# A gated FFN in seven products per tile: where its sums, its modulation rows and its kept stream are handled

## The reference, cut to what matters

```
h = rmsnorm(x, norm_ffn_g)
g = dwconv(h @ w_gate, conv_ffn_w)          # 2816 columns = 22 tiles of 128, 3 taps
v = h @ w_up
x = x + (silu(g) * v) @ w_down              # "output products"
x = rmsnorm(x, norm_final_g)
# second block: 64 columns of 128 values from the vector c
shift, scale, gate = split(silu(c) @ ada_w + ada_b, 3)      # twice, and once in two parts
h = rmsnorm(x, g) * (1 + scale) + shift
```

## Time and profile before

| | us |
|---|---|
| median of 3 runs | 2045.7 (2045.27 to 2046.42) |
| the profiled execution | 2045.31 |
| its span | 2043.5 |
| PE busy in the span | 1990.0 (97%) |
| DVE, ACT, POOL busy | 1348.1, 723.8, 1047.7 |

### The profile page before, as it was taken

How to read it: one execution, slowest core, us unless ns; L and a number is a source line. 1 busy time by engine, 2 the same in 40 slices (tenths; PEclk the granted TensorE clock), 3 DMA queues, 4 the chain that set the end, 5 groups by cost and what they waited for, 6 DMA issues and landing times.

```text
span 2043.5 us, 23948 instructions
## 1 busy us (share of the span) xinstructions
PE 1990.0 (97%) x9084; PEld 1634.0 (80%) x9084; DVE 1348.1 (66%) x1822; ACT 723.8 (35%) x1221; POOL 1047.7 (51%) x620
## 2 busy tenths in 40 slices
PE   9999999799999999999999999999999999999998
PEld 7888888577777778888888888888888878777887
DVE  6999678788888865665576454354355381497556
ACT  6323344433334344111154112112112262598112
POOL 4677828689898985211276132132132174365633
PEclk9999999899999999999999999999999999999999
DMA  4231113144545435222111021021021112010202
GB/s 159 73 114 42 52 42 134 61 177 169 191 154 206 145 121 197 83 89 117 42 40 64 31 65 49 32 71 42 31 72 42 31 42 67 11 33 21 67 17 83
DMA packets 54135, 167.56 MB, mean 82 GB/s; under 512 B 6272, under 2 KB 11536, under 8 KB 54032
## 3 DMA queue, kind: packets, MB, share of 16 engines
q1 hardware_dynamic: 41936, 127.94, 18.1%
q10 hardware_dynamic: 12096, 38.23, 5.3%
HBM read 148.30 MB, written 21.00 MB: 83 GB/s over the span
## 4 chain that ended last, share of the span: by engine, by line
PE 71%; POOL 17%; DVE 5%; issue 4%; ACT 3%; DMA 0%; POOLq 0%; DVEq 0%; SPq 0%; ACTq 0%
PE psum L914 20%; PE psum L915 20%; PE psum L916 20%; POOL w_lo L815 2%; POOL w_lo L806 2%; POOL temp L684 2%; POOL second_sum L800 2%; POOL w_lo L785 1%; POOL even_gate_lo L785 1%; ACT probs L1897 1%; POOL w_lo L810 1%; PE psum L1322 1%; POOL w_raw L802 1%; POOL w_raw L794 1%; DVE psum L1972 1%
## 5 line engine op out<-in xcount | busy, mean ns | idle before, releaser
L649 POOL TENSOR_TENSOR w_lo<-w_raw,w_hi 128x1024 fp32r<-128x1024 f32 x131 | 329.9, 2531 | 606.9 <-ACT w_hi L1422 601.6
L914 PE MATMUL psum<-norm_hi,w_hi 128*128 128x512 f32 (+1 forms) x1200 | 464.9, 387 | 0.0
L915 PE MATMUL psum<-norm_lo,w_hi 128*128 128x512 f32 (+1 forms) x1200 | 463.5, 386 | 0.0
L916 PE MATMUL psum<-norm_hi,w_lo 128*128 128x512 f32 (+1 forms) x1200 | 463.5, 386 | 0.0
L914 PEld LDWEIGHTS psum<-norm_hi,w_hi 128*128 128x128 f32 x1200 | 225.3, 188 | 46.1 <-issue 0.2
L915 PEld LDWEIGHTS psum<-norm_lo,w_hi 128*128 128x128 f32 x1200 | 225.4, 188 | 45.5 <-issue 0.2
L916 PEld LDWEIGHTS psum<-norm_hi,w_lo 128*128 128x128 f32 x1200 | 225.3, 188 | 45.4
L2031 DVE SCALAR_TENSOR_TENSOR stream<-psum,mods,stream 128x512 f32<-128x512 f32 x160 | 119.7, 750 | 172.0 <-PE psum L916 172.0
L1422 ACT CAST w_hi<-w_raw 128x1024 fp32r<-128x1024 f32 x114 | 115.9, 1048 | 218.3 <-PE psum L916 143.5
L2368 DVE TENSOR_TENSOR stream<-psum,stream 128x512 f32<-128x512 f32 x176 | 121.6, 691 | 93.8 <-PE psum L916 93.6
L2120 DVE SCALAR_TENSOR_TENSOR psum<-glu,vec,psum 128x1024 f32<-128x1024 f32 x116 | 149.6, 1290 | 4.1
(11 more groups left out here) (317 smaller groups left out, 4289.6 us busy)
## 6 DMA issues: line engine op xcount, KB each, us to landing
w_raw<-in_slabs SPq DMA_DIRECT2D x155, 512.0 KB, 3.3
ada_raw<-in_ada ACTq DMA_DIRECT2D x16, 2048.0 KB, 7.7
even_raw<-in_slabs SPq DMA_DIRECT2D x20, 512.0 KB, 4.0
ffn_y_scratch<-ffn_y SPq DMA_DIRECT2D x18, 512.0 KB, 3.5
sum_raw<-ffn_y_scratch SPq DMA_DIRECT2D x5, 1024.0 KB, 5.0
stream<-in_x SPq DMA_DIRECT2D x8, 512.0 KB, 9.3
stream_scratch<-stream SPq DMA_DIRECT2D x2, 2048.0 KB, 7.2
stream<-stream_scratch SPq DMA_DIRECT2D x2, 2048.0 KB, 12.0
```

What stands on the lines that cost most here:

```text
L649: nc.gpsimd.tensor_tensor(WL[place][:, :], RAW[at % 2][:, :], WH[place][:, :].bitcast(f32), ALU.subtract).then_inc(slab_ready, 1)
L914: nc.tensor.matmul(dst, wh, xh, start=n == 0, stop=False)
L915: nc.tensor.matmul(dst, wh, xl, start=False, stop=False)
L916: last = nc.tensor.matmul(dst, wl, xh, start=False, stop=n == len(terms) - 1)
```

## The change

- **Sums' low parts.** In the sevens POOL keeps `gate_low`, the four `weight_sums` and the low part of the second sum. The low parts of S1 and of S3/S4 (`sum_low`, `last_low`, 128x1024 each) go to DVE. `mixed_part_sum` is gone from POOL.
- **Parts from PSUM.** Three of the four `keep_part` copies are gone; DVE adds each product from its bank: seven adds a turn, each with one PSUM operand, in place of six on DVE and one on POOL.
- **Modulation rows.** 36 rows (18 turns of two) are done in turns 1 to 18, straight into `mods`; the bias is added once at the end. The other 28 are done behind output products: three each in jobs 1 to 8 (behind tiles 2, 7 and 12), four in job 9 (also behind 15). Their loads are issued by ACT inside its loop over jobs. The gains are made in the last job. POOL's `sums(POOL)` and ACT's `weight_his(POOL_SLAB, ...)` now wait for all rows.
- **`back_low`** moves from DVE to POOL, in front of the job's `lows`.
- **Stream normalised in place.** `piece(FFN, m)` is now the stream's own place, so the sums t1 to t4 are differences of its blocks: two on POOL and six on DVE in place of four on POOL and twelve on DVE. The stream is stored in eight pieces of 512 KB beforehand and `scaled` waits for the store of its piece. It comes back in eight loads, in part before the sevens end.
- The raw and gate buffers swap turns: turn 0 uses `RAW` and place 5, odd turns the spare ones. Row slab 0 may be cast a turn earlier (`row_refill`).

```
-ADA_TURNS, ADA_ROWS = 16, 4
+EARLY_TURNS, TURN_ROWS = 18, 2
+LATE_ROWS = NADA - EARLY_TURNS * TURN_ROWS
+LATE_JOBS = (1, 10)
...
-    early = (last + 2, last + 5, last + 7, last + 7, last + 7, last + 7, DOWN_TILE + 16, DOWN_TILE + 32)
+    early = (last - 5, last + 5, last + 7, last + 7, last + 7, last + 7, DOWN_TILE + 16, DOWN_TILE + 32)
...
         def piece(n, m):
+            if n == FFN:
+                return X[:, m % 8, hs(m // 8)]
...
+        def late_rows(job):
+            return [i for i in range(LATE_ROWS) if min(1 + i // 3, LATE_JOBS[1] - 1) == job]
...
             for half in range(2):
-                sp.wait_ge(dve_read, 56 + 8 * half)
-                sp.dma_start(x_scratch[:, :, hs(half)], X[:, :, hs(half)]).then_inc(x_kept, 16)
+                for k in range(0, KT, 2):
+                    sp.wait_ge(dve_read, 48 + 8 * half + k + 2)
+                    sp.dma_start(x_scratch[:, k:k + 2, hs(half)], X[:, k:k + 2, hs(half)]
+                                 ).then_inc(x_moved[(8 * half + k) // 2], 16)
...
+                nc.gpsimd.tensor_tensor(t1_raw(pair), block_of(0, 1, pair), block_of(0, 0, pair), ALU.subtract
+                                        ).then_inc(t1_made, 1)
-            for n in range(SEVENS):
-                last_low_of(n)
-                if n + 1 < SEVENS:
-                    gate_low(n + 1)
-                    weight_sums(n + 1)
-                mixed_part_sum(n)
-                if n + 1 < SEVENS:
-                    sum_lows(n + 1)
-            lows(ROW_SLAB, POOL_SLAB)
+            for n in range(1, SEVENS):
+                gate_low(n)
+                weight_sums(n)
+                second_low(n)
+            for n in range(len(JOBS)):
+                if n > 1:
+                    back_low(n)
+                lows(ROW_SLAB + 2 * n, ROW_SLAB + 2 * n + 2)
             lows(POOL_SLAB, POOL_SLAB + 2)
-            sums(POOL, (f_lo, 4))
+            sums(POOL, (ada_summed, ALL_SUMMED))
...
-                pe.wait_ge(*((part_added, 6 * n) if n else (act_read, 47)))
+                pe.wait_ge(*((part_added, 7 * n) if n else (act_read, 47)))
...
+            gate_silu(0)
             corner_cast(2, 0)
-            corner_cast(4, 0)
-            corner_cast(3, 0)
-            gate_silu(0)
+            corner_cast(2, 1)
             s1_cast(0)
-            s2_cast(0)
-            s34_cast(0)
-            y_cast(0)
             act.wait_ge(tiles, FFN_TILE + 6)
             corner_cast(1, 0)
             corner_cast(1, 1)
-            corner_cast(2, 1)
-            corner_cast(4, 1)
-            corner_cast(3, 1)
+            y_cast(0)
+            s2_cast(0)
...
+            read_second(0)
+            read_second(1)
+            s34_cast(0)
+            corner_cast(4, 0)
+            corner_cast(4, 1)
+            read_second(2)
+            read_second(3)
...
+            def load_late(i):
+                if i < 2:
+                    act.wait_ge(f_mul, FT)
+                else:
+                    act.wait_ge(ada_summed, EARLY_TURNS + i - 1)
+                act.dma_start(ada_late(i), ada_in[EARLY_TURNS * TURN_ROWS + i, :, :]).then_inc(ada_loaded[i % 2], 16)
...
-                for half in range(2):
-                    keep_part(t + 1, body(T[0], half), bank[0])
+                keep_part(t + 1, body(T[0], 1), bank[0])
...
-                act.wait_ge(f_mul, n + 2)
-                keep_part(t + 3, body(T[1], 1), bank[2])
-                if not last:
                     s2_cast(n + 1)
-                keep_part(t + 5, body(T[1], 0), bank[4])
...
             row_cast(3)
+            load_late(0)
+            load_late(1)
             for n in range(2, len(JOBS)):
                 back_cast(n)
                 row_cast(2 * n)
                 row_cast(2 * n + 1)
+                if n > 3:
+                    for i in late_rows(n - 3):
+                        if i + 2 < LATE_ROWS:
+                            load_late(i + 2)
+            for job in (len(JOBS) - 3, len(JOBS) - 2):
+                for i in late_rows(job):
+                    if i + 2 < LATE_ROWS:
+                        load_late(i + 2)
+            act.wait_ge(ada_summed, ALL_SUMMED)
             weight_his(POOL_SLAB, POOL_SLAB + 2)
...
                 gate_times_up(n + 1)
+                if n:
+                    last_low(n)
...
+                first, mixed_gate = body(T[0], 0), body(T[0], 1)
+                mixed_up, second_up = body(T[1], 0), body(T[1], 1)
+                add(first, bank[1], mixed_gate, [(tiles, t + 2), (part_kept, n + 1)])
...
+                if 1 <= n <= EARLY_TURNS:
+                    early_rows(n - 1)
+                dve.wait_ge(part_added, 7 * n + 1)
+                add(mixed_gate, bank[3], mixed_gate, [(tiles, t + 4)])
+                add(second_up, bank[2], mixed_gate, [(part_added, 7 * n + 2)])
+                add(mixed_up, bank[4], mixed_gate, [(tiles, t + 5)])
+                if n + 1 < SEVENS:
+                    sum_low(n + 1)
+                add(mixed_gate, bank[5], second_up, [(tiles, t + 6), (part_added, 7 * n + 4)])
                 gate_conv(n + 2)
+                add(second_up, bank[2], second_up, [(tiles, t + 7)])
+                add(mixed_up, bank[2], mixed_up)
...
+            def rows_behind(n, j):
+                rows = late_rows(n)
+                if j in (2, 7, 12, 15) and (2, 7, 12, 15).index(j) < len(rows):
+                    late_row(rows[(2, 7, 12, 15).index(j)])
...
-                add_rows(n, lambda j: back_low(n + 1, (j - 3) // 3) if j in (3, 6) else None)
-            dve.wait_ge(gains_done, 4)
-            add_rows(len(JOBS) - 1, lambda j: apply_early(POOL, j))
+                add_rows(n, lambda j: rows_behind(n, j))
+            add_rows(len(JOBS) - 1, gain_step)
```

More of the change, by code:

```diff
@@ L264, in build @@
         vec_ready = sem("vec_ready")
-        x_ready = [sem(f"x_ready{n}") for n in range(8)]
+        x_moved = [sem(f"x_moved{n}") for n in range(8)]
         rel_ready, sink_ready = sem("rel_ready"), sem("sink_ready")
@@ L515, in made @@
         def made(n, pair):
-            return 4 * pair + (1, 3, 2, 4)[n - 1]
+            return 2 * (2, 4, 3).index(n) + pair + 1
         def down_bank(j):
@@ L769, in _ @@
             for pair in range(2):
[L770 to L774, removed]
-                    else:
-                        gp.wait_ge(lo_done, dve_lows(FFN, 11))
-                        gp.wait_ge(pool_low, pool_lows(FFN, 11))
-                    nc.gpsimd.tensor_tensor(extra(EX_RAW, 1 - low_rows, pair),
-                                            corner(HH, low_rows, 1, pair).bitcast(f32),
-                                            corner(HL, low_rows, 1, pair).bitcast(f32), ALU.add).then_inc(corner_made, 1)
+                gp.wait_ge(norm_done, 8 + 2 * pair + 2)
+                gp.wait_ge(lo_done, 8)
+                nc.gpsimd.tensor_tensor(t1_raw(pair), block_of(0, 1, pair), block_of(0, 0, pair), ALU.subtract
+                                        ).then_inc(t1_made, 1)
             def gate_low(n):
@@ L2300, in ada_store, with ada_row @@
-            def ada_store(turn):
-                dve.wait_ge(ada_summed, turn + 1)
-                at = ADA_ROWS * turn
-                nc.vector.tensor_tensor(mods[:, at:at + ADA_ROWS], ada_sum[:, 0:ADA_ROWS],
-                                        vec[:, VEC["ada_b"] + at:VEC["ada_b"] + at + ADA_ROWS], ALU.add
-                                        ).then_inc(ada_read, 1)
-            corner_sums(0)
+            def ada_row(raw, row):
+                return nc.vector.tensor_tensor_reduce(out=raw, in0=raw, in1=C_ACT, scale=1.0, scalar=0.0, op0=ALU.mult,
+                                                      op1=ALU.add, accum_out=mods[:, row:row + 1])
@@ new lines, in early_rows, with late_row, sum_low @@
+            def early_rows(turn):
+                dve.wait_ge(*ada_arrived(turn))
+                for n in range(TURN_ROWS):
+                    ins = ada_row(ada_early(turn)[:, n, :], TURN_ROWS * turn + n)
+                ins.then_inc(ada_summed, 1)
+            def late_row(i):
+                dve.wait_ge(*ada_arrived(EARLY_TURNS + i))
+                ada_row(ada_late(i), EARLY_TURNS * TURN_ROWS + i).then_inc(ada_summed, 1)
+            def sum_low(n):
+                dve.wait_ge(s1_hi, n + 1)
+                nc.vector.tensor_tensor(WL[2][:, :], seven_raw(n)[1][:, :], WH[2][:, :].bitcast(f32), ALU.subtract
+                                        ).then_inc(s1_lo, 1)
@@ L2354, in _ @@
-                add(body(T[0], 1), bank[5], body(T[1], 1), [(tiles, t + 6), (part_added, 6 * n + 3), (part_mixed, n + 1)])
+                if 1 <= n <= EARLY_TURNS:
[6 more added lines that the diff above has]
+                    sum_low(n + 1)
```

270 lines of the change are left out of this document (139 added, 131 removed).

## The result

The changed kernel takes 2087.03 us, the median of four runs (2084.76 to 2093.27), beside 2045.94 us for the kernel before, also over four (2045.27 to 2046.42). The ratio is 1.0206, 95% interval 1.0183 to 1.0228. The forecast was 2083.5 us, range 2059 to 2099.

A forecast was written before the change was run, and what follows sets the result against it. PE was 97% busy, but POOL and DVE taking turns at SBUF inputs set the sevens' turn. Span 2043.5 - 22.3 + 46.8 + 10.8 + 2.9 = 2081.7 us, so 2083.5 us forecast, range 2059 to 2099.

The forecast's parts named there:

- Which rows are late, and why: Output products: third rows of jobs 1 and 3 to 7, their loads issued behind casts that wait for PE.
- Their size: Output products: stalls of 13.8 us in job 1 and 6.6 in each of jobs 3 to 7, 46.8 us lost.
- The clock: Slow granted clock on PE behind six stalls: 1.8 us each, 10.8 us lost (bounds 1.8 and 10.8).
- Job 2: Output products: its late loads are issued in a pass whose slabs don't wait for PE, cost 0.
- The turn: Sevens: one turn takes 19.9 us against 20.8, set by POOL and DVE taking turns, not by PE's 19.1.
- The walk of an alternating port: Sevens: POOL and DVE instructions with two SBUF inputs strictly alternate, first to ask going first; gives 19.9 us a turn.
- Before turn 0: DVE's work up to turn 0's add behind product 5: that add at 396.6 against 404.43, 7.8 us earlier.
- the gain up to the output products: Everything before the output products: they start at 774.2 against 796.5, a gain of 22.3 us.
- The normalisation: Before the first turn: DVE's lows, now with two SBUF inputs, wait for POOL's; +4 us on PE (bounds 0 and 6).
- The last job: End of the output products: casts and POOL's lows behind row 27 delay the sums of squares, PE stands 2.9 us.
- The total: Whole kernel: span 2043.5 - 22.3 + 46.8 + 10.8 + 2.9 = 2081.7 us, time 2083.5 us.
- Rival 1: Output products: third rows' loads are hidden, 57.6 us of stall and clock go, 2025.9 us; chance 0.08.

The follow-up runs named there:

- Experiment 1: Changed kernel with ACT issuing third rows' loads ahead of the casts that wait for a job's end (job 1: between its casts): 2040.44 us, ratio 0.9978 to the kernel before.
- experiment 2: Changed kernel with only job 1's late load moved between its two casts, jobs 2 to 7 left as they were: 2082.99 us, ratio 1.0172 to the kernel before.
- experiment 3: Changed kernel with ACT casting weight sum S1 before S2 in each turn of the sevens: 2068.2 us, ratio 1.0117 to the kernel before.

## Why the prediction was right, and where it was not, step by step

- **Which rows are late, and why.** Right. Six stalls, at the ends of jobs 1, 3, 4, 5, 6 and 7, the adds behind the third row, the row behind its load, the load behind a cast that waits for PE. Experiment 1 removes the cause and the stalls.
- **Their size.** 39.5 us for 46.8: 13.1 for 13.8 and 26.4 for 33.0. The term mis-sized is the issue behind both casts: it goes out as the first one starts to run, 1.9 us earlier. In jobs 3, 5 and 7 that changed little (6.2 for 6.6), since the row still came behind POOL's second low, as forecast. In jobs 4 and 6 it let the row in ahead of that low, and the wait is 3.9.
- **The clock.** 12.1 for 10.8, above the upper bound. Behind the short waits too it is near the lower level, and each stall costs 1.75 to 2.24 us where I had 1.8.
- **Job 2.** "0" was right in the changed kernel and wrong as a statement on its load: the stall of job 1 hid a wait of 3.0 us, 6 with its clock, as experiments 1 and 2 show.
- **The turn.** 19.94 for 19.9. The walk of an alternating port held, and also its remark that the S1 cast misses the better order by little: experiment 3 reaches 19.1 by exchanging two casts.
- **Before turn 0.** This step failed in size: the add at 402.09 for 396.6. I priced nine DVE instructions at 1.14 to 1.2 each and set POOL's three lows of that stretch beside them for nothing, although the same rule was used two paragraphs before. Measured 16.8 for 10.3; the gain up to the output products was 15.9, not 22.3.
- **The normalisation.** 3.0 for 4. **The last job.** 6.3 for 2.9 (bounds 0 and 4): the wait is 3.3 us longer, and the slow clock behind it, 3.0, had been left out.
- **The total.** The gain was smaller by 6.4 us, the loss in the output products smaller by 2.1 (58.4 for 60.5). The difference, 4.3, is the error of the span (2086.1 for 2081.7), up to rounding. That the total is this close is in part luck: the stalls came out 7.3 us under, the clock and the last job 4.7 over, and the gain 6.4 under.

Rival 1 (no stalls) is what experiment 1 builds. Its price, 2025.9, assumed the gain of 22.3; with 15.9, job 2's wait and its clock (6.1) and the last job's 3.4 us more it would be 2041.8, beside 2041.93 of the profiled execution and a median of 2040.44.

## What to carry to other kernels

When a load is moved behind another instruction in an engine's order, ask what that instruction waits for: a cast that waits for the end of a job ties the next data to that end, and the load's own 3 to 4 us, with what stands behind it, become PE's idle time, six times over. Where VectorE and GpSimd both read pairs from SBUF, write down who asks first at each meeting. An exchange of two casts made the output products begin 17.1 us earlier here, as much as the whole change had won up to that point (15.9). And price a stall's neighbours as if that stall were gone: job 2's load was covered here by nothing but job 1's stall.

## What the runs showed of the hardware that was not expected

- A transfer on ACT's queue was issued at 883.47, while the first of the two casts ahead of it in the program ran from 883.38 to 884.43, and the second had not begun.
- The same port race gives PE waits of 3.90 or 6.20 us at like places of one execution, as the load lands 3.2 or 3.7 to 4.1 us after its issue.
- A wait of 3.19 us in turn 0 was followed by a granted clock of 0.50 over 4 us, and one of 3.05 in experiment 1 likewise; a wait of 3.15 in turn 1, 14 us after the first, left it at 1.00. Waits of up to 1.5 us in the sevens of before left it at 1.00.
- Behind equal waits of 6.20 us the slow stretch lasted 3.1 us in one execution and 5.6 in another, 1.5 and 2.7 us of PE's time.
